# Attention scores from split queries and keys: two full-precision products per step become six single-pass ones

## The chip, the cores and the metric

The kernel runs on 1 core of one Trainium2 chip. The time is the device time in microseconds of that core, the median of three executions. Before the change: 3159.59 us (3159.53 to 3167.47).

## The reference, cut to what matters

The program computes two transformer blocks for 1024 tokens of width 1024, in float32. The change is in the second block, in its differential attention: 4 heads, each with two maps (two sets of 64-wide queries and keys), whose softmax weights are subtracted.

```python
for blk in range(t // Q_BLOCK):                    # 8 blocks of 128 queries
    start, end = blk * Q_BLOCK, (blk + 1) * Q_BLOCK
    qb = q[:, :, :, start:end].astype(jnp.float32) # (B, heads, 2 maps, 128, 64)
    kb = k[:, :, :, :end].astype(jnp.float32)
    s = jnp.einsum('bhmqd,bhmkd->bhmqk', qb, kb) * scale
    ...                                            # distance bias, causal mask
    p = jax.nn.softmax(s, axis=-1)
    a = p[:, :, 0] - lam * p[:, :, 1]
    outs.append(jnp.einsum('bhqk,bhkd->bhqd', a, vf[:, :, :end]))
```

Only the einsum that makes `s` is computed in another way by the change.

## The kernel before

Each engine has its own program in one hand-written order; semaphores join them. Most of TensorE's time goes to dense products of 128x512 columns in which float32 operands have been cut into a high part (rounded to the type fp32r) and a low part (the rest): high by high, low by high and high by low, three matmuls that each pass the array once (L436, L476 to L478). ScalarE cuts the high part of each weight tile (`WH`, L1167), GpSimd subtracts to get the low one (`WL`, L2530).

The attention stage (`pe_diff`, `act_diff`, `dve_diff`) has 32 steps n = 0 to 31: head h = n // 8, query block i = n % 8. A step works on w = 128 (i+1) keys. The step's engine order is software pipelined:

- TensorE: `scores(n)`, some pieces of dense work ("ticks": the projections of the next head and early gate products, L436), `values(n-2)` (transposes of the weights, L957), more ticks, `outs(n-3)` (products with the values, L974), and once a head the transposes of `turn` (L984).
- VectorE: `scores(n)` (L2205: add the bias, write to `PD`, take the row maximum; one instruction per map; then L2208), `weights(n-1)` (L2214 to L2218), `values(n-2)` (the copy to `AT`, L2227), and at some blocks `scale`, `norm` (a chain of 15 short instructions, then L2251) and `turn` (the copy to `SD`, L2258).
- ScalarE: `scores(n)` (the exponentials, L1468), the evacuations of the dense work (`QD`, `KD`, `VX`, `EG` by L1172) each followed by a cut of `WH` (L1167), part of `AT` (L1478), and once a head 8 squares (L1493).

Queries and keys lie transposed in `QD` and `KD`, map 0 in partitions 0 to 63 and map 1 in 64 to 127. `scores(n)` multiplies, for each map and each PSUM bank of up to 512 keys, 64 rows of float32. The profile shows each such product as two matmul records. PSUM banks are handed out in turn by `claim`, which waits until the last reader has drained them.

Of the kernel before, what the change touches and what calls it, by code (L numbers as in the profile page):

```python
# [7 lines left out]
F = mybir.dt.float32  # L8
R = mybir.dt.float32r
I32 = mybir.dt.int32  # L10
ACT = mybir.ActivationFunctionType
# [238 lines left out]
def build(nc, D, out):  # L250
    plan, order1, order2 = weight_plan()
    with ExitStack() as ctx:
        def sb(name, kb, shape, dt=F):
            return nc.alloc_sbuf_tensor_at(name, shape, dt, offset=BASE + int(kb * KB))

        def sem(name):
            return ctx.enter_context(nc.semaphore(name))
# [25 lines left out]
        ln_in, ln_ab, ln_sc, ln_g, ln_x = (sem(n) for n in (  # L283
            "ln_params_landed", "ln_stats", "ln_scaled", "ln_gained", "ln_out"))
        g_ylo2 = sem("s5_out_later_low_cut")
        t_hi, n_x = sem("token_tile_high_cut"), sem("last_tile_out")
        f_cv, f_act, f_hi, f_lo = (sem(n) for n in ("ffn_conv_begun", "ffn_activated", "ffn_mid_high_cut", "ffn_mid_low_cut"))
        xb_out, out_done = [sem(f"x_stored{t}") for t in range(8)], sem("out_stored")
# [91 lines left out]
        AT = sb("AT", 180, [128, 2, 1024])  # L380
        YD = sb("YD", 188, [128, 2, 8, 128])
        SD = sb("SD", 196, [128, 2, 1024])

        DDs = [sb("DD0", 116, [128, 1024]), sb("DD1", 120, [128, 1024])]
        YG = sb("YG", 116, [128, 8, 256])
# [520 lines left out]
        def finish(steps):  # L906
            for _ in steps:
                pass
# [16 lines left out]
        def pe_diff(e):  # L925
            def project(h):
                yield from pe_feature_steps(e, ("dq", h), "w_in_2", 128 * h)
                yield
                yield from pe_feature_steps(e, ("dk", h), "w_in_2", 512 + 128 * h)
                yield  # L930
                yield from pe_values_steps(e, ("dv", h), 1024 + 128 * h)

            def scores(n):
                h, i = diff_steps[n]
                hb, w = h % 2, 128 * (i + 1)
                if i == 0:
                    for key in (("dq", h), ("dk", h)):
                        e.wait_ge(lots[key].drained, lots[key].ndrained)
                for m in range(2):
                    rr = slice(64 * m, 64 * m + 64)  # L940
                    u = claim(e, ("ds", n, m), 1 if w <= 512 else 2)
                    for c in range(2):
                        if w > 512 * c:
                            last = e.matmul(PS[:, u.b + c, 0:min(512, w - 512 * c)], QD[rr, hb, 128 * i:128 * i + 128],  # L944
                                            KD[rr, hb, 512 * c:min(512 * c + 512, w)], start=True, stop=True)
                    last.then_inc(u.full, 1)

            def values(n):
                h, i = diff_steps[n]
                for g in range(0, i + 1, 4):  # L950
                    k = min(4, i + 1 - g)
                    u = claim(e, ("dt", n, g))
                    if g == 0:
                        e.wait_ge(d_p, n + 1)
                    for j in range(k):
                        c = 128 * (g + j)
                        last = e.transpose(PS[:, u.b, 128 * j:128 * j + 128], PD[:, n % 3, 0, c:c + 128], ident[:, :])  # L957
                    last.then_inc(u.full, 1)

            def outs(n):  # L960
                h, i = diff_steps[n]
                if i == 0:
# [13 lines left out]
                last.then_inc(d_o, 1)  # L976

            def turn(h):
                if h == 3:
                    bk.let(lots["do", 3])  # L980
                u = claim(e, ("dy", h), 2)
                e.wait_ge(d_y, h + 1)
                for i in range(8):
                    last = e.transpose(PS[:, u.b + i // 4, 128 * (i % 4):128 * (i % 4) + 128], YD[:, h % 2, i, :], ident[:, :])  # L984
                last.then_inc(u.full, 1)

            def beside(h):
                if h < 3:
                    yield from project(h + 1)
                yield from pe_early(e, BESIDE_HEAD[h])  # L990
                if h == 3:
                    yield from pe_feature_steps(e, "glr", "glr", 0)

            pe_open(e, "x2", [(("dq", 0), "w_in_2", 0), (("dk", 0), "w_in_2", 512), ((("dv", 0), "x"), "w_in_2", 1024)])
            pe_turn_values(e, ("dv", 0))
            fill = iter(())
            for n in range(36):
                if n < 32:
                    h, i = diff_steps[n]
                    if i == 0:  # L1000
                        finish(fill)
                        fill = beside(h)
                    scores(n)
                tick(fill, ticks(n)[0])
                if 2 <= n < 34:
                    values(n - 2)
                tick(fill, ticks(n)[1])
                if 3 <= n < 35:
                    outs(n - 3)
                    if diff_steps[n - 3][1] == 2 and diff_steps[n - 3][0]:  # L1010
                        turn(diff_steps[n - 3][0] - 1)
            finish(fill)
            finish(pe_gated_keys(e, 0))
            turn(3)
# [429 lines left out]
        def act_diff(e):  # L1444
            def project(h):
# [10 lines left out]
                if h < 2:  # L1456
# [3 lines left out]
                yield from act_values_steps(e, ("dv", h), VD[:, hb, :, :],  # L1460
                                            [(d_o, 8 * h - 8)] if h >= 2 else [(xb_out[4 + h], 16)])

            def scores(n):
                h, i = diff_steps[n]
                S, w = SMD[:, n % 4, :], 128 * (i + 1)
                e.wait_ge(d_s, n + 1)
                for m in range(2):
                    e.activation(PD[:, n % 3, m, 0:w], PD[:, n % 3, m, 0:w], ACT.Exp, bias=S[:, 2 + m:3 + m],  # L1468
                                 accum_out=S[:, 4 + m:5 + m]).then_inc(d_e, 1)
# [45 lines left out]
                e.activation(L(9), L(6), ACT.Ln).then_inc(lb_b, 1)  # L1515

            finish(project(0))
            fill = iter(())
            for n in range(36):
                if n == 4:  # L1520
                    bounds()
                if n < 32:
                    h, i = diff_steps[n]
                    if i == 0:
                        finish(fill)
                        fill = beside(h)
                    scores(n)
                tick(fill, ticks(n)[0])
                if 2 <= n < 34:
                    values(n - 2)  # L1530
                tick(fill, ticks(n)[1])
                if 3 <= n < 35 and diff_steps[n - 3][1] == 7:
                    take(diff_steps[n - 3][0])
                if 4 <= n and diff_steps[n - 4][1] == 7:
                    square(diff_steps[n - 4][0])
# [655 lines left out]
        def dve_diff(e):  # L2191
# [68 lines left out]
            def bounds():  # L2260
# [10 lines left out]
                e.wait_ge(lb_b, 3)  # L2271
                e.tensor_scalar(L(8), L(8), -63 * math.log(2.0), None, ALU.add).then_inc(dve, cv.up())

            e.wait_ge(cst3, 16)
            e.tensor_copy(LV[:, :, :].rearrange("p a c -> p (a c)"), LVI[:, :]).then_inc(dve, cv.up())
            e.wait_ge(dl_in, 16)
            e.tensor_tensor(DL[:, 0:64], DL[:, 0:64], DL[:, 64:128], ALU.mult).then_inc(dve, cv.up())
            then(e.tensor_tensor, DL[:, 64:128], DL[:, 128:192], DL[:, 192:256], ALU.mult)
# [3 lines left out]
            then(e.tensor_scalar, LM[:, 5:6], LM[:, 4:5], -0.2, None, ALU.add)  # L2282
            then(e.tensor_scalar, LM[:, 6:7], cols[:, C_NW:C_NW + 1], 0.8, None, ALU.mult)
            e.wait_ge(dve, cv.n)
            for n in range(36):
                if n == 4:
                    bounds()
                if n < 32:
                    scores(n)
                if 1 <= n < 33:  # L2290
                    weights(n - 1)
                if 2 <= n < 34:
                    values(n - 2)
                if 3 <= n:
                    h, i = diff_steps[n - 3] if n < 35 else (4, 0)
                    if i == 7:
                        scale(h)
                    if i == (1 if h < 4 else 0) and h:
                        norm(h - 1)
                    if i == 2 and h:  # L2300
                        turn(h - 1)
# [893 lines left out]
```

## Time and profile before

| | |
|---|---|
| median of three runs | 3159.59 us |
| profiled execution | 3164.47 us, span 3162.3 us |
| TensorE matmul busy | 3049.1 us, 96% |
| VectorE, ScalarE, GpSimd busy | 39%, 29%, 33% |
| attention stage | about 1212 to 1500 us of the span |

The span is the time from the first to the last instruction in the trace. An engine's share of busy time is a mean over all stages. Matmul durations overlap, since each includes the array's fill and drain: what a matmul costs in a stream is the distance from its start to the next one's. The chain that ended last, which is followed back from release to release, tells what a delay would cost.

### The profile page before, as it was taken

Reading aid. Unit: us, or ns where it says so; the run is one execution under the profiler, and the core shown is the slowest. Engines: PE = TensorE matmul, PEld = TensorE weight load, DVE = VectorE, ACT = ScalarE, POOL = GpSimd, SP = SyncE. Lnnn points to the kernel's source line nnn. Section 1 sums busy time; section 2 is a strip of 40 time slices with the busy share of each in tenths; the row PEclk is TensorE's granted clock in tenths of the full one; section 3 lists DMA queues with packets and bytes.
Section 4 is the critical chain, followed back from the end, with each engine's and each line's share of the span. In section 5 each row is a group of like instructions: output and inputs, shape, how many; then the busy total and the mean of one; then the engine's idle time right before and its main releaser. Section 6 shows DMA issues by size and latency. Waiting matters only on the chain.

```text
span 3162.3 us, 35710 instructions
## 1 busy us (share of the span) xinstructions
PE 3049.1 (96%) x14710; PEld 2504.5 (79%) x14710; DVE 1243.5 (39%) x2353; ACT 913.8 (29%) x1340; POOL 1046.5 (33%) x514
## 2 busy tenths in 40 slices
PE   8998999999999999999999999999999999999998
PEld 7776788888888876777777777788888788888886
DVE  8836642112122155555346544532454111112115
ACT  3223342211212134333424533433322212111111
POOL 4443345232322353111223332331223633333335
PEclk9898999999999999999999999999999999999999
DMA  6331311121111122111111111124331112111111
GB/s 208 87 113 62 95 46 48 46 67 40 54 54 40 54 64 86 53 47 61 41 34 41 54 54 48 33 80 147 127 139 41 53 54 62 52 47 47 51 43 54
DMA packets 70897, 207.62 MB, mean 66 GB/s; under 512 B 11376, under 2 KB 19968, under 8 KB 70720
## 3 DMA queue, kind: packets, MB, share of 16 engines
q1 hardware_dynamic: 70736, 205.34, 20.3%
q8 instruction: 117, 1.92, 0.2%
q14 instruction: 44, 0.36, 0.0%
HBM read 172.54 MB, written 32.77 MB: 65 GB/s over the span
## 4 chain that ended last, share of the span: by engine, by line
PE 86%; DVE 4%; ACT 3%; POOL 3%; issue 3%; DMA 0%; SPq 0%; ACTq 0%; DVEq 0%; POOLq 0%
PE PS L436 47%; PE PS L476 7%; PE PS L477 7%; PE PS L478 7%; PE PS L756 3%; PE PS L1067 3%; POOL WL L2530 2%; PE PS L944 1%; PE PS L974 1%; PE PS L502 1%; PE PS L563 1%; PE PS L859 1%; PE PS L857 1%; PE PS L858 1%; DVE s L1739 1%
## 5 line engine op out<-in xcount | busy, mean ns | idle before, releaser
L2530 POOL TENSOR_TENSOR WL<-WR,WH 128x1024 fp32r<-128x1024 f32 x241 | 580.1, 2414 | 1870.5 <-ACT WH L1167 1870.2
L436 PE MATMUL PS<-XH,WH 128*128 128x512 f32 x2176 | 690.6, 399 | 16.8 <-DVE XL L1778 9.1
L436 PE MATMUL PS<-XL,WH 128*128 128x512 f32 x2176 | 674.2, 391 | 0.0
L436 PE MATMUL PS<-XH,WL 128*128 128x512 f32 x2176 | 672.9, 390 | 0.0
L436 PEld LDWEIGHTS PS<-XH,WH 128*128 128x128 f32 x2176 | 397.2, 189 | 109.2 <-issue 25.8
L436 PEld LDWEIGHTS PS<-XH,WL 128*128 128x128 f32 x2176 | 409.8, 188 | 87.7
L436 PEld LDWEIGHTS PS<-XL,WH 128*128 128x128 f32 x2176 | 410.0, 188 | 87.3
L1167 ACT ACTIVATE WH<-WR 128x1024 fp32r<-128x1024 f32 x241 | 253.2, 1055 | 665.7 <-PE PS L478 443.4
L476 PE MATMUL PS<-WH,HH 128*128 128x512 f32 x736 | 287.2, 390 | 2.5 <-POOL HL L2562 2.5
L478 PE MATMUL PS<-WH,HL 128*128 128x512 f32 x736 | 287.0, 390 | 0.0
L477 PE MATMUL PS<-WL,HH 128*128 128x512 f32 x736 | 286.8, 390 | 0.0
L2159 DVE TENSOR_TENSOR CT<-CT,PS 128x1024 f32<-128x1024 f32 x54 | 65.9, 1221 | 459.1 <-ACT CT L1388 310.9
L2172 DVE TENSOR_TENSOR XF<-XF,PS 128x512 f32<-128x512 f32 x160 | 110.0, 687 | 313.2 <-PE PS L478 313.2
L476 PEld LDWEIGHTS PS<-WH,HH 128*128 128x128 f32 x736 | 138.5, 188 | 31.8 <-POOL HL L2562 2.9
L476 PE MATMUL PS<-WH,XH 128*128 128x512 f32 x384 | 154.5, 402 | 9.4 <-DVE XL L2026 5.4
L477 PEld LDWEIGHTS PS<-WL,HH 128*128 128x128 f32 x736 | 138.6, 188 | 28.8
L478 PEld LDWEIGHTS PS<-WH,HL 128*128 128x128 f32 x736 | 138.5, 188 | 28.9
L477 PE MATMUL PS<-WL,XH 128*128 128x512 f32 x384 | 151.7, 395 | 0.0
L478 PE MATMUL PS<-WH,XL 128*128 128x512 f32 x384 | 151.6, 395 | 0.0
L2562 POOL TENSOR_TENSOR HL<-CT,HH 128x1024 fp32r<-128x1024 f32 x54 | 129.3, 2395 | 7.6 <-ACT HH L1394 7.6
L2153 DVE SCALAR_TENSOR_TENSOR CT<-PS,cols,CT 128x1023 f32<-128x1023 f32 x22 | 28.2, 1283 | 238.3 <-ACT CT L1381 238.3
L2381 DVE COPY_PREDICATED ST<-LV,PS 128x512 f32<-128x512 uint8 x128 | 85.8, 727 | 76.1 <-PE PS L1067 75.7
(349 smaller groups left out, 3991.8 us busy)
## 6 DMA issues: line engine op xcount, KB each, us to landing
WR<-in_weights SPq DMA_DIRECT2D x241, 512.0 KB, 3.6
gates<-EG SPq DMA_DIRECT2D x18, 512.0 KB, 5.2
EI<-gates SPq DMA_DIRECT2D x18, 512.0 KB, 4.7
BR<-brbuf SPq DMA_DIRECT2D x12, 512.0 KB, 6.4
RAWX<-in_xT SPq DMA_DIRECT2D x8, 512.0 KB, 7.2
spill<-STQ SPq DMA_DIRECT2D x16, 256.0 KB, 2.2
RX<-in_x SPq DMA_DIRECT2D x8, 512.0 KB, 6.1
xbuf<-XF SPq DMA_DIRECT2D x8, 512.0 KB, 2.6
```

The costliest lines, as they stand in the source:

```text
L436: last = e.matmul(PS[:, u.b + h, :], w, x[:, k, 512 * h:512 * h + 512], start=k == 0 and w is w1 and x is xh, stop=k == nk - 1 and w is w2)
L476: e.matmul(PS[:, u.b, :], a, wh[:, k, :], start=j == 0 and k == 0, stop=False)
L477: e.matmul(PS[:, u.b, :], a, wl[:, k, :], start=False, stop=False)
L478: last = e.matmul(PS[:, u.b, :], c, wh[:, k, :], start=False, stop=j == len(vs) - 1 and k == 1)
L756: last = e.matmul(PS[:, u.b + h, :], w[:, k, :], x[:, k, 512 * h:512 * h + 512], start=k == 0 and w is wh and x is XH, stop=k == 7 and w i ...
L1067: last = e.matmul(PS[:, us[g][hh].b, 128 * (i % 4):128 * (i % 4) + 128], kl[rows[hh], c], kr[rows[hh], c], start=True, stop=True)
L1167: e.activation(WH[:, v % NSPL, :], WR[:, v % NRAW, :], ACT.Copy).then_inc(w_hi, 1)
L2159: e.tensor_tensor(X, X, bank(u, 2), ALU.mult).then_inc(u.drained, 1)
L2172: e.tensor_tensor(x, x, bank(u), ALU.add).then_inc(u.drained, 1)
L2381: e.copy_predicated(o, LV[:, n:n + 1, :].to_broadcast([128, 4, 128]), four(u)).then_inc(u.drained, 1)
L2530: e.tensor_tensor(WL[:, v % NSPL, :], WR[:, v % NRAW, :], WH[:, v % NSPL, :].bitcast(F), ALU.subtract).then_inc(w_lo, 1)
L2562: e.tensor_tensor(HL[:, v % 5, :], CT[:, v % 2, :], HH[:, v % 5, :].bitcast(F), ALU.subtract).then_inc(f_lo, 1)
```

## The change

Before each step's scores, ScalarE copies the new block of 128 keys and 128 queries to high parts (`KH`, `QH`, type fp32r), and VectorE subtracts these from `KD` and `QD` to get low parts (`KL`, `QL`, which lie where `KD` and `QD` lay). `split(n+1)` stands on ScalarE ahead of the exponentials of step n; `lows(n+1)` stands on VectorE behind the maxima of step n. TensorE's `scores(n)` claims the banks of both maps, waits for `lows(n)`, and issues for each bank three products (high queries by high keys, low by high, high by low) for map 0 and map 1 in turn. The wait for the drained projections moves from TensorE to ScalarE's `split`. The copy of the mask levels gets a semaphore of its own, since `KH` and `QH` reuse its input's place.

```diff
+        QL, KL = sb("QL", 116, [128, 2, 1024], R), sb("KL", 124, [128, 2, 1024], R)
+        KH = sb("KH", 218.75, [128, 1024], R)
+        QH = [sb("QH0", 218, [128, 128], R), sb("QH1", 205, [128, 128], R)]
...
-                for m in range(2):
-                    rr = slice(64 * m, 64 * m + 64)
-                    u = claim(e, ("ds", n, m), 1 if w <= 512 else 2)
-                    for c in range(2):
-                        if w > 512 * c:
-                            last = e.matmul(PS[:, u.b + c, 0:min(512, w - 512 * c)], QD[rr, hb, 128 * i:128 * i + 128],
-                                            KD[rr, hb, 512 * c:min(512 * c + 512, w)], start=True, stop=True)
-                    last.then_inc(u.full, 1)
+                us = [claim(e, ("ds", n, m), 1 if w <= 512 else 2) for m in range(2)]
+                e.wait_ge(d_lo, n + 1)
+                kl, ql = KL[:, hb, :], QL[:, hb, :]
+                for c in range(-(-w // 512)):
+                    k = slice(512 * c, min(512 * c + 512, w))
+                    for p, (x, y) in enumerate(((QH[n % 2][:, :], KH[:, k]), (ql[:, q], KH[:, k]), (QH[n % 2][:, :], kl[:, k]))):
+                        for m in range(2):
+                            rr = slice(64 * m, 64 * m + 64)
+                            last = e.matmul(PS[:, us[m].b + c, 0:k.stop - k.start], x[rr], y[rr], start=p == 0, stop=p == 2)
+                            if p == 2 and k.stop == w:
+                                last.then_inc(us[m].full, 1)
...
+            def split(n):                        # ScalarE
...
+                if n >= 2:
+                    read = lots["ds", n - 1 if i == 0 else n - 2, 1]
+                    e.wait_ge(read.full, read.nfull)
+                e.activation(KH[:, c], KD[:, h % 2, c], ACT.Copy)
+                e.activation(QH[n % 2][:, :], QD[:, h % 2, c], ACT.Copy).then_inc(d_hi, 1)
...
             finish(project(0))
+            split(0)
...
+                    if n < 31:
+                        split(n + 1)
                     scores(n)
...
+            def lows(n):                         # VectorE
...
+                e.wait_ge(d_hi, n + 1)
+                for L, X, H in ((KL, KD, KH[:, c]), (QL, QD, QH[n % 2][:, :])):
+                    last = e.tensor_tensor(L[:, h % 2, c], X[:, h % 2, c], H.bitcast(F), ALU.subtract)
+                last.then_inc(d_lo, 1)
...
+            lows(0)
             for n in range(36):
...
                     scores(n)
+                    if n < 31:
+                        lows(n + 1)
```

TensorE, the first step of the stage before (one row is one product of a map; w is 128):

```order
L502 MATMUL PS<-ident,VX 128x128 x3
L944 MATMUL PS<-KD,QD 128x128 [waits bank6_drained,bank0_drained]
L944 MATMUL PS<-KD,QD 128x128 [waits bank6_drained]
L436 MATMUL PS<-XH,WH 128x512 [waits weight_low_cut,bank0_drained]
L436 MATMUL PS<-XH,WH 128x512
```

The same place now (`QH_143` and `QH_144` are the two query buffers, in turn; all line numbers have moved a little):

```order
L506 MATMUL PS<-ident,VX 128x128 x3
L948 MATMUL PS<-KH,QH_143 128x128 [waits diff_block_low_cut,bank6_drained]
L948 MATMUL PS<-KH,QH_143 128x128
L948 MATMUL PS<-KH,QL 128x128 x2
L948 MATMUL PS<-KL,QH_143 128x128 x2
L440 MATMUL PS<-XH,WH 128x512 [waits weight_low_cut,bank0_drained]
L440 MATMUL PS<-XH,WH 128x512
```

Two products have become six, and the first of them waits for VectorE's subtractions.

ScalarE, the start of the stage now; before, the table load and the exponentials (L1468 then) stood directly behind the two copies to `VD`:

```order
L1171 ACTIVATE WH<-WR 128x1024 [waits bank4_full,weight_landed0]
L1436 ACTIVATE VD<-PS 128x512 [waits bank4_full,x_stored4]
L1436 ACTIVATE VD<-PS 128x512 [waits bank5_full]
L1479 ACTIVATE KH<-KD 128x128 [waits bank0_drained,bank6_drained,levels_copied]
L1480 ACTIVATE QH_143<-QD 128x128
L1479 ACTIVATE KH<-KD 128x128
L1480 ACTIVATE QH_144<-QD 128x128
L1487 ACT_TABLE_LOAD
L1487 ACTIVATE PD,SMD<-PD,SMD 128x128 [waits diff_scores_max]
```

The first split stands behind the work that ScalarE did there already, and the first scores now wait for it.

VectorE now, at step 28 (the fifth block of the last head), where the subtractions stand between the maxima (L2227 and L2230 here) and the weights of the step before (from L2236):

```order
L2227 ISA PD,SMD<-PS,AL 128x640 [waits bank6_full]
L2227 ISA SMD 128x1
L2230 TENSOR_SCALAR SMD<-SMD 128x2 [waits bank6_drained]
L2302 TENSOR_TENSOR KL<-KD,KH 128x128 [waits diff_block_high_cut]
L2302 TENSOR_TENSOR QL<-QD,QH_144 128x128
L2236 RECIPROCAL SMD<-SMD 128x2 [waits diff_exp]
L1761 TENSOR_TENSOR SMD<-SMD,LM 128x1 [waits vector_step]
```

The weights, the copy to `AT` and the norm behind them now also wait until ScalarE has split the next block.

## Rows read from the trace of the kernel before

**Rows 1.** Page: the span, and the chain that ended last by engine.

```profile
span 3162.3 us, 35710 instructions
PE 86%; DVE 4%; ACT 3%; POOL 3%; issue 3%; DMA 0%; SPq 0%; ACTq 0%; DVEq 0%; POOLq 0%
```

**Rows 2.** Chain of the stage: start us, us, engine and line, instructions.

```profile
1276.98 0.42 PE PS L944 x4
...
1282.48 0.63 PE PS L944 x4
...
1289.88 0.85 PE PS L944 x4
...
1296.99 1.06 PE PS L944 x4
...
1301.22 2.77 PE PS L436 x12
...
1304.21 1.29 PE PS L944 x8
...
1472.46 1.92 PE PS L944 x8
```

**Rows 3.** Timeline, weight loads of step 6: start, us, engine line op.

```profile
1264.79 0.31 PEld L944 LDWEIGHTS PS<-KD,QD 64*128 64x128 f32 x4
1265.32 0.20 PEld L944 LDWEIGHTS PS<-KD,QD 64*128 64x128 f32 x2 [0.23 <-issue]
1265.75 0.20 PEld L944 LDWEIGHTS PS<-KD,QD 64*128 64x128 f32 x2 [0.23 <-issue]
```

**Rows 4.** Single lines: durations in ns, min/median/max.

```profile
L2251 DVE TENSOR_TENSOR YD<-YD,SH x4: 1224/1224/1224, 1312.4 to 1510.7; 128x1024 f32<-128x1024 f32 x4
L1478 ACT ACTIVATE AT<-PS x16: 255/424/598, 1260.8 to 1494.9; 128x128 f32<-128x128 f32 x4, 128x256 f32<-128x256 f32 x4, 128x384 f32<-128x384 f32 x4, 128x512 f32<-128x512 f32 x4
L2489 DVE TENSOR_TENSOR BL<-BR,BH x12: 1211/1214/2590, 2173.7 to 2295.9; 128x1024 fp32r<-128x1024 f32 x12
```

**Rows 5.** Timeline, start of the stage.

```profile
1211.31 1.06 PE L502 MATMUL PS<-ident,VX 128*128 128x128 f32 x8 [1.21 <-ACT VX L1172]
1212.03 1.08 ACT L1432 ACTIVATE VD<-PS 128x512 f32<-128x512 f32 x2
1212.18 2.39 POOL L2530 TENSOR_TENSOR WL<-WR,WH 128x1024 fp32r<-128x1024 f32 x1 [2.98 <-ACT WH L1167]
1212.30 0.49 PE L944 MATMUL PS<-KD,QD 64*128 64x128 f32 x4
```

**Rows 6.** Timeline, step 25.

```profile
1422.65 2.38 POOL L2530 TENSOR_TENSOR WL<-WR,WH 128x1024 fp32r<-128x1024 f32 x1 [15.07 <-ACT WH L1167]
1422.76 2.30 DVE L2208 TENSOR_SCALAR SMD<-SMD 128x2 f32<-128x2 f32 x1
...
1427.96 0.64 PEld L957 LDWEIGHTS PS<-ident,PD 128*128 128x128 f32 x6 [0.49 <-DVE AT L2227]
```

**Rows 7.** Timeline, step 28.

```profile
1448.24 0.48 DVE L2216 TENSOR_SCALAR PD<-PD,SMD 128x512 f32<-128x512 f32 x1
...
1449.55 0.81 ACT L1468 ACTIVATE PD<-PD,SMD 128x640 f32<-128x640 f32 x1
```

**Rows 8.** Timeline, step 30.

```profile
1460.27 3.29 PE L944 MATMUL PS<-KD,QD 64*128 64x512 f32 x8
1460.45 1.28 DVE L2258 TENSOR_SCALAR SD<-PS,LM 128x1024 f32<-128x1024 f32 x1 [2.12 <-PE PS L984]
...
1461.79 0.29 PEld L944 LDWEIGHTS PS<-KD,QD 64*128 64x128 f32 x2 [0.37 <-DVE SD L2258]
1462.21 1.09 DVE L2205 CUSTOM_DVE_ANT_0 PD<-PS,AL 128x896 f32<-128x896 f32 x1 [0.48 <-PE PS L944]
...
1463.60 1.09 DVE L2205 CUSTOM_DVE_ANT_0 PD<-PS,AL 128x896 f32<-128x896 f32 x1 [0.28 <-PE PS L944]
...
1468.06 0.77 PE L957 MATMUL PS<-ident,PD 128*128 128x128 f32 x5 [1.54 <-ACT EG L1172]
```

**Rows 9.** Stretches: from:to, us, busy us of PE, PEld, DVE, ACT, POOL; then granted clock, DMA.

```profile
1160.00:1172.50 12.50, 9.84 (x51) 7.92 (x49) 8.45 (x35) 9.11 (x14) 9.07 (x4) 1.00 0.09 22
1172.50:1175.90 3.40, 3.35 (x8) 2.71 (x9) 1.51 (x4) 0.44 (x2) 3.40 (x3) 0.50 0.75 240
```

**Rows 10.** Timeline of TensorE around that fall of the clock.

```profile
1168.34 1.94 PE L502 MATMUL PS<-ident,XF 128*128 128x128 f32 x16 [0.44 <-POOL XF L2536]
1172.55 0.77 PE L756 MATMUL PS<-XH,WH 128*128 128x512 f32 x1 [2.28 <-DVE XL L2076]
```

More of the change, by code:

```diff
@@ L285, in build @@
         g_ylo2 = sem("s5_out_later_low_cut")
+        lv_set, d_hi, d_lo = sem("levels_copied"), sem("diff_block_high_cut"), sem("diff_block_low_cut")
         t_hi, n_x = sem("token_tile_high_cut"), sem("last_tile_out")
@@ L934, in scores @@
                 h, i = diff_steps[n]
[L935 to L938, printed above, removed]
-                for m in range(2):
-                    rr = slice(64 * m, 64 * m + 64)
-                    u = claim(e, ("ds", n, m), 1 if w <= 512 else 2)
-                    for c in range(2):
-                        if w > 512 * c:
-                            last = e.matmul(PS[:, u.b + c, 0:min(512, w - 512 * c)], QD[rr, hb, 128 * i:128 * i + 128],
-                                            KD[rr, hb, 512 * c:min(512 * c + 512, w)], start=True, stop=True)
-                    last.then_inc(u.full, 1)
+                hb, w, q = h % 2, 128 * (i + 1), slice(128 * i, 128 * i + 128)
+                us = [claim(e, ("ds", n, m), 1 if w <= 512 else 2) for m in range(2)]
[9 more added lines that the diff above has]
+                                last.then_inc(us[m].full, 1)
             def values(n):
@@ L1461, in project @@
                                             [(d_o, 8 * h - 8)] if h >= 2 else [(xb_out[4 + h], 16)])
+            def split(n):
+                h, i = diff_steps[n]
+                c = slice(128 * i, 128 * i + 128)
+                if n == 0:
+                    e.wait_ge(lv_set, 1)
+                if i == 0:
+                    for key in (("dq", h), ("dk", h)):
+                        e.wait_ge(lots[key].drained, lots[key].ndrained)
+                if n >= 2:
[3 more added lines that the diff above has]
+                e.activation(QH[n % 2][:, :], QD[:, h % 2, c], ACT.Copy).then_inc(d_hi, 1)
             def scores(n):
@@ L2272, in bounds @@
                 e.tensor_scalar(L(8), L(8), -63 * math.log(2.0), None, ALU.add).then_inc(dve, cv.up())
+            def lows(n):
+                h, i = diff_steps[n]
+                c = slice(128 * i, 128 * i + 128)
+                e.wait_ge(d_hi, n + 1)
+                for L, X, H in ((KL, KD, KH[:, c]), (QL, QD, QH[n % 2][:, :])):
+                    last = e.tensor_tensor(L[:, h % 2, c], X[:, h % 2, c], H.bitcast(F), ALU.subtract)
+                last.then_inc(d_lo, 1)
             e.wait_ge(cst3, 16)
-            e.tensor_copy(LV[:, :, :].rearrange("p a c -> p (a c)"), LVI[:, :]).then_inc(dve, cv.up())
+            e.tensor_copy(LV[:, :, :].rearrange("p a c -> p (a c)"), LVI[:, :]).then_inc(lv_set, 1)
+            e.wait_ge(lv_set, 1)
             e.wait_ge(dl_in, 16)
```

## The prediction

> **What bounds the kernel now.** I read the page's chain first: TensorE is 86% of the chain that ended last [rows 1]. Then the same chain over the attention stage (1212 to 1500 us): it goes from one group of matmuls to the next, the scores (L944) among them, so that a microsecond taken from the scores or put in front of them is one of the kernel's, as long as no other engine comes late. Last the timelines at the start of the stage and in its last head, where the chain leaves TensorE [rows 5 to 8].
>
> The reader is to see three things. The scores of a step with i = 0, 1, 2, 3 take 0.42, 0.63, 0.85 and 1.06 us, with i = 4 and 7 1.29 and 1.92 us, from their start to that of the next dense matmul [rows 2]. So 128 more keys cost both maps together 0.21 us. The weight loads of step 6 come in twos, one per map, every 0.43 us [rows 3]: the two maps run side by side already, though the program issues all of map 0 first. Alternating them therefore gives nothing by itself. And a full-height single-pass matmul of 512 columns costs 2.77 / 12 = 0.23 us [rows 2], against 0.43 us for a record of the float32 product.
>
> **TensorE's own part.** A step is now 0.10 us of first load, then per bank two records of 0.111, 0.215, 0.322 or 0.4285 us (for 128 to 512 keys), then 0.10 us until a full-height matmul may follow: this gives 0.42, 0.63, 0.85, 1.06, 1.29, 1.49, 1.71, 1.92 us, as the rows have it. After, a bank takes three single-pass records. At 512 keys I take 0.227 us each (the 0.23 above). Narrow ones cannot beat the load of 128 weight columns, 0.11 us (four loads, in two pairs one behind the other, take 0.31 us, and one pair 0.20 [rows 3]); I take 0.109 for 128 keys, 0.12 for 256, 0.174 for 384. Steps i = 0 to 7 then take 0.53, 0.57, 0.73, 0.89, 1.22, 1.25, 1.41, 1.57 us: changes of +0.11, -0.07, -0.12, -0.18, -0.07, -0.25, -0.30, -0.35, in sum -1.23 us per head and **-4.9 us** for four heads. Where map 1's banks come late, both end at the same distance from that release, so these steps save the same. No row shows single-pass products of 64 rows side by side. From one side: half a float32 record, 0.214 us at all widths in proportion, -7 us. From the other: the maps run one behind the other, which adds three records per bank, 6.5 us per head, +26 us on top of -4.9. I take the pair side by side, since the nearest row, the float32 pair [rows 3], does so.
>
> **Added work on the other engines.** Per step two ScalarE copies of 128x128 (0.26 us, the shortest of L1478 [rows 4]; with overlap about 0.5 us) and two VectorE subtractions of 128x128. L2251, the same operation at 1024 columns, takes 1.22 us [rows 4]; at about 1.05 ns a column and a fixed 0.15 us, 128 columns take 0.28 us, the two about 0.5 us. Over 32 steps that is 16 us on each, of engines that are 39% and 29% busy. ScalarE does the split while it waits for the maxima, and VectorE has several us between steps in heads 0 to 2: there it is hidden, and if that cover went it would cost up to 0.5 us a step. It shows in three places.
>
> *Start of the stage, +2.8 us.* TensorE issues the first scores at 1212.30 us. Now `split(0)` stands behind the two copies to `VD`, which end at 1213.1 [rows 5], so ScalarE is done at 1213.6. The first subtraction reads two tiles in SBUF while GpSimd's cut of `WL` runs until 1214.57 [rows 5]. In the trace a short VectorE instruction behind such a cut lasts 2.30 us until the cut ends [rows 6], and the subtraction of the same form, L2489, once takes 2.59 instead of 1.21 us [rows 4]. So 1214.6, plus 0.5, and TensorE starts at about 1215.1. Without blocking it would be 1214.1, +1.8 us; nothing bounds it below that, since the copies to `VD` come first. (The Trainium skill, page "SBUF — State Buffer", section "Who interferes with whom", states that a tensor_tensor with both inputs in SBUF contends with GpSimd's reads and that the later one waits for the whole instruction. By that rule the start costs the 2.8 us, without it 1.8; the trace agrees with the rule through L2489.)
>
> *The last head, +3.9 us.* Its steps have few ticks, so that VectorE is nearly the bound. Step 25: `L2208` sits out a GpSimd cut [rows 6], then come the weights of a 1024-wide step and the copy to `AT`, for which TensorE's transposes wait at 1427.96; the subtractions put 0.5 to 0.6 us in front of them: +0.6. Step 28: ScalarE's 8 squares end just before its exponentials at 1449.55 [rows 7]; `split(29)` now follows them, to about 1450.4 with the 0.2 us by which this place has already slipped, and `lows(29)` ends at 1451.1. The weights that began at 1448 us [rows 7] begin there, about 3 us late. Behind them stand `AT`, the norm chain, the maxima of step 29, `lows(30)`, more weights, and the copy to `SD`. This moves `SD` from ending at 1461.74 to about 1463.6. In step 30 map 1 waits for it [rows 8]; map 0 does not, and its maximum starts at 1462.21, before map 1 is done. Now both maps are claimed first, so both start at 1463.7 and end together at 1465.1: the maxima of map 0 start at 1465.2 and end with those of map 1 (1.09 us each, [rows 8]) at 1467.6 instead of 1464.9. Behind them are the exponentials, the copy to `EG`, and TensorE's transposes, which wait for it at 1468.06 [rows 8]. They slip to 1470.8: +2.7 in all, which eats the 1.2 us that steps 23 to 30 had saved and 2.7 more, together 3.9.
>
> *Steps 14 and 22, +0.3 us*: the same loss of map 0's head start, 0.75 us on VectorE, of which 0.6 has cover.
>
> **The clock.** In the old order TensorE idles 1.21 us, does 8 transposes and goes on. Now another 2.8 us of idling follow. The nearest case is at 1172.5 us: 16 transposes, 2.28 us idle [rows 10], and the granted clock is 0.50, that is 1.2 GHz, for the next 3.4 us [rows 9]. In those 3.4 us 8 matmuls run instead of 15: 7 x 0.23 = 1.6 us; a stretch may be twice as long. I count **+2.0 us**; the other end is 0.
>
> **Sum.** -4.9 + 2.8 + 3.9 + 0.3 + 2.0 = +4.1 us. On the profiled execution (3164.47 us, span 3162.3) this makes 3168.6. That execution is 4.9 us above the median of the runs shown, so I put the difference on the median: 3159.6 + 4.1 = **3163.7 us**. A measurement of this kernel can hardly tell 0.3% (9.5 us) from no change.
>
> **Rivals.**
> 1. *Cover holds everywhere but at the start* (no slip of the last head, no fall of the clock). For it: VectorE is idle 2.12 us before `SD` [rows 8], which could take up more than I let it. Against it: the squares stand directly in front of the split. -4.9 + 2.8 = -2.1: 3157.5 us.
> 2. *The single-pass maps do not run side by side.* Place: the 36 banks' worth of records of each map. Price +26 us, and it decides as soon as the third product costs more than the pass it saves, that is, if the pair takes over 0.29 us per 512 keys. For it: no row shows the pair; against it: the float32 pair [rows 3]. 4.1 + 26 = +30: 3190 us.
> 3. *Each 64-row product costs as much as a float32 record* (the single pass is not had at this height or at narrow widths). Records now cost 7.74 us per head; three for two adds half, 15.5 us in four heads, instead of saving 4.9: +24.5 us, 3184 us. If only the 128-key products (eight times three) cost a full-width float32 one, 0.43 instead of 0.109, it is +7.7 us: 3171 us.
>
> Another reading of the trace concerns whether loads hide. (The Trainium skill, page "TensorE: Matmul & The Clock Gate", section "The mechanism", states that a weight load overlaps matmuls in flight only when the row group differs. By it each added product of a pair would show 0.11 us of load, 48 of them, +5 us.) The loads of step 6 start 0.43 us apart, which is the passes alone [rows 3], so I leave this price out of the sum; it has 0.03 of the chance, inside my forecast's band.
>
> **Chances.** My forecast with its details somewhat off (3154 to 3169) 0.62; rival 1 0.17; rival 2 0.06; rival 3 in either form 0.10, half of it within 0.3% of before or little over; something not seen 0.05. Faster by over 0.3% needs more than twice what TensorE can save in my sum: 0.05. Slower by over 0.3% (above 3169): rivals 2 and 3 and the upper tail of the forecast (two slow stretches of the clock, more slips): 0.19. Within: 0.76. Range 3152 to 3177 us, with most of rival 1 and the milder half of rival 3; rivals 2 and 3 in full are left out.
>
> **What would show it.** TensorE: the step with i = 7 takes 1.57 instead of 1.92 us, with loads in twos; if it takes about 2.9, rival 2; if 2.8 with records of 0.43, rival 3. The step with i = 0 gets longer. Start: the first scores about 2.8 us later behind the transposes, the first subtraction ending with GpSimd's cut. Last head: the copy to `AT` 0.6 us later at step 25, `SD` of step 30 about 2 us later, the transposes behind `EG` 2.7 us later than the chain before. Clock: a stretch at 0.50 directly behind the first scores. The prediction is wrong if the records are not near 0.23 us at 512 columns, or if VectorE's delay reaches TensorE in heads 0 to 2.

## The result, and the profile after

The changed kernel takes 3171.46 us (median of 16 executions, 3166.32 to 3173.23), against 3159.56 us for the kernel before on the same chip (16 executions, 3149.16 to 3168.51): a ratio of 1.0033 with a 95% interval of 1.0020 to 1.0046, so about 10 us slower (6 to 15). I had forecast 3163.7 us, 4.1 more than before, with a range of 3152 to 3177. The measured time is inside the range, but above the band of 3154 to 3169 us to which I had given 0.62; times above 3169 us had 0.19.

The profiled execution took 3169.16 us against 3164.47. The page, its span and the chain by engine, which answer to [rows 1]:

```profile
span 3167.3 us, 36060 instructions
...
PE 84%; DVE 4%; ACT 4%; issue 3%; POOL 3%; DMA 0%; SPq 0%; DVEq 0%; ACTq 0%; POOLq 0%
```

TensorE's matmuls are busy 3039.5 us instead of 3049.1, and yet the span is 5.0 us longer. In the chain its share falls by two points: less of what decides the end is its work.

The chain of the stage (start us, us, engine and line, instructions) answers to [rows 2]. These are the steps with i = 0 to 4 and the first one with i = 7:

```profile
1263.16 1.59 PE PS L948 x12
...
1274.95 0.48 PE PS L948 x6
...
1280.49 0.55 PE PS L948 x6
...
1287.83 0.72 PE PS L948 x6
...
1294.78 0.90 PE PS L948 x6
...
1301.87 1.18 PE PS L948 x12
```

0.42, 0.63, 0.85, 1.06, 1.29 and 1.92 us have become 0.48, 0.55, 0.72, 0.90, 1.18 and 1.59. The weight loads of one such step (timeline of the loads) answer to [rows 3]:

```profile
1263.09 0.18 PEld L948 LDWEIGHTS PS<-KH,QH 64*128 64x128 f32 x2
1263.20 0.19 PEld L948 LDWEIGHTS PS<-KH,QL 64*128 64x128 f32 x2
1263.44 0.19 PEld L948 LDWEIGHTS PS<-KL,QH 64*128 64x128 f32 x2
1263.67 0.19 PEld L948 LDWEIGHTS PS<-KH,QH 64*128 64x128 f32 x2
```

They come in twos, 0.23 us apart at 512 keys where the float32 ones were 0.43 apart. That is what the pass of one product of 512 columns costs, so the loads of 0.19 us stay hidden and the two maps do run side by side.

The start of the stage (timeline), beside [rows 5]:

```profile
1206.32 1.07 PE L506 MATMUL PS<-ident,VX 128*128 128x128 f32 x8 [1.21 <-ACT VX L1176]
1207.04 1.08 ACT L1436 ACTIVATE VD<-PS 128x512 f32<-128x512 f32 x2
1207.20 2.35 POOL L2565 TENSOR_TENSOR WL<-WR,WH 128x1024 fp32r<-128x1024 f32 x1 [2.95 <-ACT WH L1171]
1208.02 0.31 ACT L1479 ACTIVATE KH<-KD 128x128 fp32r<-128x128 f32 x1
...
1208.63 1.07 DVE L2302 TENSOR_TENSOR KL<-KD,KH 128x128 fp32r<-128x128 f32 x1 [3.18 <-ACT QH L1480]
...
1209.61 0.28 DVE L2302 TENSOR_TENSOR QL<-QD,QH 128x128 fp32r<-128x128 f32 x1
...
1210.04 0.33 PE L948 MATMUL PS<-KH,QH 64*128 64x128 f32 x2 [2.65 <-DVE QL L2302]
```

The first scores wait 2.65 us, in the order that the prediction gave: the copies to `VD`, the split, a first subtraction that ends only 0.15 us behind GpSimd's cut (1208.63 + 1.07 = 1209.70 against 1207.20 + 2.35 = 1209.55), a second of 0.28 us.

Two stretches at half clock appear in the stage, one directly behind those scores and one in the last head. The third row is outside the stage. Columns as in [rows 9]:

```profile
1210.60:1214.00 3.40, 3.40 (x8) 2.71 (x9) 1.07 (x7) 1.28 (x6) 0.00 (x0) 0.50 0.40 149
1466.60:1470.00 3.40, 2.80 (x9) 2.45 (x10) 0.69 (x1) 1.77 (x3) 1.83 (x1) 0.50 0.00 0
1978.60:1982.00 3.40, 3.40 (x14) 3.01 (x13) 1.33 (x2) 2.51 (x5) 2.78 (x2) 0.50 0.00 1
```

The last head, beside [rows 7] and [rows 8], from the timeline of steps 28 to 30:

```profile
1440.91 0.49 PE L948 MATMUL PS<-KH,QH 64*128 64x512 f32 x2 [1.42 <-ACT EG L1176]
...
1445.20 0.40 ACT L1512 ACTIVATE JK<-YD,SH 128x128 f32<-128x128 f32 x1
...
1445.60 0.29 ACT L1479 ACTIVATE KH<-KD 128x128 fp32r<-128x128 f32 x1
...
1446.12 0.29 DVE L2302 TENSOR_TENSOR KL<-KD,KH 128x128 fp32r<-128x128 f32 x1 [2.01 <-ACT QH L1480]
...
1447.99 0.55 DVE L2249 COPY AT<-PS 128x384 f32<-128x384 f32 x1
...
1448.64 0.50 PE L948 MATMUL PS<-KH,QH 64*128 64x512 f32 x2 [1.37 <-issue]
...
1453.49 0.95 DVE L2227 CUSTOM_DVE_ANT_0 PD<-PS,AL 128x768 f32<-128x768 f32 x1
1453.63 0.66 PE L961 MATMUL PS<-ident,PD 128*128 128x128 f32 x4 [0.72 <-DVE SMD L2227]
...
1458.70 1.28 DVE L2280 TENSOR_SCALAR SD<-PS,LM 128x1024 f32<-128x1024 f32 x1 [1.40 <-PE PS L988]
...
1461.73 1.09 DVE L2227 CUSTOM_DVE_ANT_0 PD<-PS,AL 128x896 f32<-128x896 f32 x1 [1.74 <-PE PS L948]
...
1462.75 1.09 DVE L2227 CUSTOM_DVE_ANT_0 PD<-PS,AL 128x896 f32<-128x896 f32 x1
...
1467.20 1.33 PE L961 MATMUL PS<-ident,PD 128*128 128x128 f32 x5 [2.66 <-ACT EG L1176]
```

The reader should follow the delay downwards. The last of the squares (L1512) starts at 1445.20. Only behind it, at 1445.60, comes the split, and VectorE had idled 2.01 us for it. Its weights come late, so the copy to `AT` ends at 1448.54, and the scores of step 29 start 0.10 us later: TensorE stood still 1.37 us ahead of them, for a bank that this copy drains. "issue" there means that the trace names no releaser; but the transposes that the copy reads and one map of the scores of step 29 raise the same semaphore when they end, so they use the same bank. Then the transposes behind those scores wait 0.72 us for the first of VectorE's maxima of step 29. At `SD` it is VectorE that waits for TensorE (1.40 us on L988), and both maps of step 30 start when `SD` is done.

### The profile page after: what moved, and what is told of

It is laid out like the page before. It is cut to its first block, busy times and chain, and to the rows that moved or that the text cites. A ratio compares the mean times of both kernels' runs of the same rounds, so it can differ in the third digit from the quotient of the medians.

```text
span 3167.3 us, 36060 instructions
## 1 busy us (share of the span) xinstructions
PE 3039.5 (96%) x14806; PEld 2511.2 (79%) x14806; DVE 1257.3 (40%) x2417; ACT 926.4 (29%) x1404; POOL 1049.2 (33%) x514
## 4 chain that ended last, share of the span: by engine, by line
PE 84%; DVE 4%; ACT 4%; issue 3%; POOL 3%; DMA 0%; SPq 0%; DVEq 0%; ACTq 0%; POOLq 0%
PE PS L440 46%; PE PS L480 7%; PE PS L481 7%; PE PS L482 7%; PE PS L760 3%; PE PS L1071 3%; POOL WL L2565 2%; PE PS L948 1%; PE PS L978 1%; PE PS L506 1%; PE PS L567 1%; PE PS L863 1%; PE PS L861 1%; PE PS L862 1%; DVE s L1761 1%
```

## Where the difference arises

I read the same marks in each trace: the last dense product ahead of the stage, the first dense product behind `scores(0)` (start), step 24 (heads 0 to 2), and the end of the stage. The sums are worked out from start times of the same matmuls; those taken for the last two marks start some 0.5 us ahead of the first product of step 24 and 0.8 us ahead of the first dense one behind the stage. "Half clock" is the time at 0.50 within the stage. The last three columns are differences to before in us: the stage; everything from the stage's first mark to the end of the span, against the mean of the four traces of before; and the whole kernel by its ratio.

| kernel | start | heads 0-2 | last head | half clock | stage | from the stage on | kernel |
|---|---|---|---|---|---|---|---|
| before (4 traces) | 3.0 | 208.2 | 79.0 | 0 | 0 | 0 | 0 |
| after | 5.8 | 206.3 | 83.4 | 6.8 | +5.2 | +9.2 | +10.4 |
| after again | 6.1 | 206.8 | 83.6 | 10.2 | +6.3 | +7.3 | +7.9 |
| work without saving | 6.0 | 210.4 | 81.6 | 6.8 | +7.8 | +6.7 | +6.3 |
| first split alone | 6.0 | 210.4 | 79.0 | 6.8 | +5.3 | +4.1 | +4.1 |
| maps one after the other | 6.2 | 211.6 | 81.4 | 6.8 | +8.9 | +10.5 | +8.2 |
| the three edits together | 3.1 | 209.5 | 79.4 | 0 | +1.8 | +3.8 | +4.1 |
| earlier first split | 3.1 | 204.8 | 83.6 | 3.4 | +1.2 | +2.6 | +0.3 |
| split ahead of the squares | 6.1 | 206.8 | 79.9 | 6.8 | +2.6 | +4.2 | +1.3 |
| both, still alternating | 3.1 | 204.8 | 81.5 | 3.4 | -0.9 | +0.4 | 0.0 |
| float32 alternated | 3.0 | 208.9 | 80.3 | 0 | +1.9 | +2.0 | +1.3 |

The last column is uncertain by 3 to 5 us either way. The stage explains it within 2.5 us in all but one row, that of the first trace after the change.

That the first two spans differ by just the stage's 5 us is chance. The program ahead of the stage has the same 5440 matmuls in every kernel, and the stage's first mark falls between 1201 and 1211 us, at 1204.7 after the change and at 1209.7 before: this part was 5.0 us shorter. What follows, counted from the first dense product behind the stage, was 4.8 us longer (1666.3 against 1661.5 us). It too has the same matmuls everywhere, and what moves it is mostly stretches at half clock. It takes 1660.3, 1661.5, 1661.5 and 1665.9 us in the four traces of before and 1663.3 to 1666.3 in the seven with single-pass scores.

## The experiments

**Work without saving** (e_work). The splits, subtractions and waits stay; the scores are the two float32 products again. The low parts are written over the high ones and used by nothing.

```diff
-                e.wait_ge(d_lo, n + 1)
...
+                    if m == 0:
+                        e.wait_ge(d_lo, n + 1)
...
-                for L, X, H in ((KL, KD, KH[:, c]), (QL, QD, QH[n % 2][:, :])):
-                    last = e.tensor_tensor(L[:, h % 2, c], X[:, h % 2, c], H.bitcast(F), ALU.subtract)
+                for X, H in ((KD, KH[:, c]), (QD, QH[n % 2][:, :])):
+                    last = e.tensor_tensor(H, X[:, h % 2, c], H.bitcast(F), ALU.subtract)
```

> All the splitting stays (two ScalarE copies and two VectorE subtractions a step, TensorE's wait for them), but TensorE multiplies the unsplit float32 queries and keys, map 0 first, as before the change; the subtractions write over the high parts, which nothing reads. My theory (single-pass products save about 4.9 us in the attention stage, the added work costs 2.8 us at its start and about 4 us in the last head, and the clock adds some): the stage is 5 us longer than with the change and 9 to 11 us longer than before. Rival A (the products are what costs, the splitting is hidden): the stage takes what it did before. Rival B (what was lost lies outside the stage, where half-clock stretches fall): the stage differs from before by under 3 us.

Measured: ratio 1.0020 (1.0011 to 1.0028). The stage is 7.8 us longer than before, less than the 9 to 11 expected, and 1.5 to 2.6 us longer than with the change instead of 5. Heads 0 to 2 take 210.4 us, the same as in the next kernel, which has no work there: the added work is hidden in them. In the last head it costs 2.6 us and not 4: this kernel keeps map 0's lead and has no half-clock stretch there.

**First split alone** (e_start_only). As e_work, but `split`, `lows` and the wait for n = 0 only.

```diff
-                    if n < 31:
-                        split(n + 1)
...
-                    if n < 31:
-                        lows(n + 1)
...
+                    if m == 0 and n == 0:
+                        e.wait_ge(d_lo, 1)
```

> The kernel before, with only the first step's split and subtractions and TensorE's wait for them; no other step is split, all products are float32 as before. My theory: the first scores start about 3 us later behind the transposes, a stretch of half clock follows them in the profile, and the stage is 4 to 5 us longer than before. Rival (TensorE's later waits absorb the delay): under 1.5 us longer.

Measured: ratio 1.0013 (0.9999 to 1.0026). The start costs 3.0 us and the last head nothing. Heads 0 to 2 are 2.2 us longer, through 6.8 us at half clock behind the first scores: the one wait brings two costs.

**Maps one after the other** (e_seq). All three products of map 0, then those of map 1, each with its own claim.

```diff
-                for c in range(-(-w // 512)):
...
+                for m in range(2):
+                    rr = slice(64 * m, 64 * m + 64)
+                    u = claim(e, ("ds", n, m), 1 if w <= 512 else 2)
```

> The change, but map 0's products are all issued ahead of map 1's, with the banks of map 1 claimed only then. My theory (the two maps run side by side in whatever order they are issued, and map 0's lead is worth something where map 1's banks come late): a step with i = 7 takes 1.6 us as with the change, the weight loads come in twos, and the last head's step 30 has its first maximum 1 us earlier; the time is 0 to 2 us below the change's. Rival (only alternation makes them run side by side): the step with i = 7 takes 2.9 us, and the time is about 26 us above.

Measured: ratio 1.0026 (1.0015 to 1.0036). The expectation (1.6 us at i = 7, and a time at or below the change's) was wrong: the stage is 2.6 to 3.7 us longer than with the change. TensorE's timeline at step 7, then three pieces of the chain:

```profile
1271.81 0.50 PE L949 MATMUL PS<-KH,QH 64*128 64x512 f32 x1
1272.15 0.39 PE L949 MATMUL PS<-KH,QL 64*128 64x512 f32 x1
1272.38 0.39 PE L949 MATMUL PS<-KL,QH 64*128 64x512 f32 x1
1272.38 0.61 PE L949 MATMUL PS<-KH,QH 64*128 64x512 f32 x2
...
1273.65 0.39 PE L949 MATMUL PS<-KL,QH 64*128 64x512 f32 x1
```

```profile
1271.88 2.15 PE PS L949 x12
...
1284.24 0.49 PE PS L949 x6
...
1289.79 0.55 PE PS L949 x6
```

Map 1's first product starts at 1272.38, together with map 0's third, 0.57 us after map 0's first. The step ends alone with map 1's last products: 2.15 us instead of 1.59. Steps with i = 4 to 7 take 1.75, 1.83, 1.98 and 2.15 us (1.18, 1.24, 1.43 and 1.59 when alternating), those with i = 0 to 3 are as short as before. With six products of map 0 ahead of it map 1 comes late; with three, or with the four records of the float32 version, it does not. In heads 0 to 2 this costs 4.8 us (211.6 against the 206.8 of c_after, which has the same 6.8 us at half clock there). In the last head it takes some 2 us less than alternating (81.4 against 83.4 and 83.6), but without the half-clock stretch that both alternating traces have in it.

**The three edits together** (e_best): e_seq with the next two.

> The change with three mends: the first split stands on ScalarE behind the copy to KD instead of behind the copies to VD; in the steps with squares the next split stands ahead of them; map 0's products are issued first, its banks claimed alone. My theory: all of the start's 3 us and its half-clock stretch go, and most of the last head's 4 us, so the stage is 3 to 5 us shorter than before the change and about 9 shorter than with it. Rival (VectorE's subtractions themselves, 0.5 us a step, carry the loss of the last head): the stage is within 1 us of before.

Measured: ratio 1.0013 (1.0000 to 1.0026). The stage is 1.8 us longer than before, where 3 to 5 us shorter was expected. The start (3.1 us) and the last head (79.4) are repaired; the late map 1 costs 4.7 us in heads 0 to 2 (209.5 - 204.8). What map 0's lead gives back in the last head, less what the late map 1 costs there, is 0.5 us (79.4 against the 79.9 of e_squares, neither with a half-clock stretch in it).

**After again** (c_after), unchanged.

> The change as it is, once more, beside the others on the same chip. My theory: the stage costs about 5 us more than before in the profile, and where half-clock stretches fall outside the stage differs from one execution to the next; the time is 4 to 12 us above before. Rival (the stage's loss seen in the first profile was an accident of the clock): the stage is within 2 us of before.

Measured: ratio 1.0025 (1.0012 to 1.0039). Start and last head agree with the first trace within 0.4 us. The stretch behind the first scores is 6.8 us long instead of 3.4 and costs 2.0 us instead of 1.5 (206.8 and 206.3 against 204.8 of the kernel below that has none).

**Earlier first split** (e_start). `split(0)` directly behind the evacuation of the keys.

```diff
                 act_evac(e, lots["dk", h], KD[:, hb, :], 2)
+                if h == 0:
+                    split(0)
...
             finish(project(0))
-            split(0)
```

> The change with one mend: the first split stands on ScalarE behind the copy to KD instead of behind the copies to VD. My theory: the first scores follow the transposes as before the change, the half-clock stretch there goes, and by the end of head 2 the stage is 3 to 4 us ahead of before; the last head still gives back about 4; the stage comes out 4 to 5 us shorter than with the change. Rival (GpSimd's cut blocks the subtraction wherever it stands, or the delay is only moved): under 1.5 us shorter.

Measured: ratio 1.0001 (0.9986 to 1.0016). Its timeline, where the split stands 5.7 us ahead of the first scores:

```profile
1198.98 0.30 ACT L1481 ACTIVATE KH<-KD 128x128 fp32r<-128x128 f32 x1
...
1202.81 0.29 DVE L2303 TENSOR_TENSOR KL<-KD,KH 128x128 fp32r<-128x128 f32 x1
...
1203.66 1.06 PE L506 MATMUL PS<-ident,VX 128*128 128x128 f32 x8 [1.21 <-ACT VX L1176]
...
1204.66 0.33 PE L948 MATMUL PS<-KH,QH 64*128 64x128 f32 x2
```

The scores follow the transposes without a wait, the clock does not fall there, and heads 0 to 2 show the saving bare: 208.2 - 204.8 = 3.4 us. The last head still costs 4.6. The stage is 4.0 to 5.1 us shorter than with the change, as expected.

**Split ahead of the squares** (e_squares). In steps 12, 20 and 28 the next split is issued before the squares instead of behind them.

```diff
-                    if n < 31:
+                    if n < 31 and n not in (12, 20, 28):
                         split(n + 1)
...
                 if 4 <= n and diff_steps[n - 4][1] == 7:
+                    if n < 31:
+                        split(n + 2)
                     square(diff_steps[n - 4][0])
```

> The change with one mend: in steps 12, 20 and 28 the split of the next block stands ahead of the squares instead of behind them. My theory (the squares in front of the split delay the subtractions, and by them VectorE's chain up to the copy to SD): SD of step 30 ends 2 us earlier against the scores of step 27 than with the change, and the last head gives back 1.5 to 2.5 us less. Rival (the subtractions themselves fill VectorE in the last head): under 0.7 us less.

Measured: ratio 1.0004 (0.9992 to 1.0017). The last head is 0.9 us longer than before instead of 4.4. It is 3.5 to 3.7 us shorter than with the change, more than the 1.5 to 2.5 expected, because no half-clock stretch falls in it. The chain runs on TensorE from step 28 to step 30 without the wait ahead of step 29; what stays is the 1.50 us until `SD` is done, ahead of the scores of step 30:

```profile
1438.25 1.26 PE PS L948 x12
...
1444.61 1.24 PE PS L948 x12
...
1448.85 0.66 PE PS L961 x4
...
1453.82 1.50 issue
1455.31 1.48 PE PS L948 x11
```

How far each mark lies behind the kernel before, in us, counted from the start of step 24 in each trace (1421.62 before, 1417.41 after, 1414.75 here):

| mark | before, at | after | split ahead of the squares |
|---|---|---|---|
| end of the scores, step 28 | 1446.01 | +0.3 | +0.4 |
| end of the scores, step 29 | 1452.64 | +1.5 | +0.1 |
| transposes behind the scores of step 29 | 1455.43 | +2.4 | +0.3 |
| end of the scores, step 30 | 1463.57 | +2.2 | +0.1 |
| transposes behind `EG`, step 30 | 1468.06 | +3.4 | +1.2 |
| end of the scores, step 31 | 1474.38 | +4.4 | +0.9 |

So the place behind the squares costs 2.1 us (3.35 - 1.23 at the transposes behind `EG`). The other 1.2 us stay in both: they arise in step 30, where both maps now end together and the maxima of both follow. The half-clock stretch adds some 1.3 us by the end of step 31 (4.4 - 3.4, and 0.3 that the step itself saves); this kernel has none there.

**Both, still alternating** (e_best2).

> The change with both mends, the first split early and the splits ahead of the squares, and the two maps alternating as in the change. The run with map 0 first showed that with two banks per map the maps then overlap only from the third product on (2.15 us instead of 1.59 at i = 7), so alternation stays. My theory: the stage is 2 to 5 us shorter than before the change and 7 to 9 us shorter than with it; the kernel is 0 to 5 us faster than before. Rival (the lost lead of map 0 carries the last head's loss): it gives back 3 us there all the same, and the stage is within 1 us of before.

Measured: 3159.31 us, ratio 1.0000 (0.9985 to 1.0015). The stage is 0.9 us shorter than before. This is the best form of the changed kernel, and it only draws level: 3.4 us saved in heads 0 to 2, 2.5 lost in the last head, where a half-clock stretch has come back. The rival of the expectation described this better than my theory of 2 to 5 us: about 1.2 of the 2.5 us are map 0's lost lead, the rest the stretch.

**Float32 alternated** (e_alt32). The kernel before with both claims first and the float32 products of the two maps in turn, nothing split.

```diff
+                us = [claim(e, ("ds", n, m), 1 if w <= 512 else 2) for m in range(2)]
+                for c in range(-(-w // 512)):
+                    k = slice(512 * c, min(512 * c + 512, w))
+                    for m in range(2):
```

> The kernel before with one part of the change alone: the banks of both maps are claimed first and the float32 products of the two maps alternate bank by bank; nothing is split. My theory (they ran side by side anyway, and all that this part does is to take away map 0's lead where map 1's banks come late): steps with i = 7 stay at 1.92 us, and in the last head the transposes behind EG come 0.5 to 1.5 us later against the scores of step 27; the stage is 0.5 to 2 us longer than before. Rival (alternation is a gain by itself): the steps with i = 4 to 7 get shorter by 0.2 us or more.

Measured: ratio 1.0004 (0.9992 to 1.0016). The step with i = 7 keeps its 1.92 us, and the stage is longer by 0.6 us in heads 0 to 2 and 1.3 in the last head. For the float32 products the alternation gains nothing and costs map 0's lead: the transposes behind `EG` in step 30 come 1.3 us later than before, counted from step 24, nearly the 1.2 us that both kernels of the table above keep. TensorE's wait there:

```profile
1465.33 0.77 PE L958 MATMUL PS<-ident,PD 128*128 128x128 f32 x5 [2.66 <-ACT EG L1173]
```

That wait is 2.64 to 2.67 us in all six traces in which the maps alternate, and 1.53 to 1.55 in the eight in which map 0 goes first. So the long wait comes from the two maps going together and not from the splitting. The half-clock stretch of the last head goes with it: four of the six traces have one, none of the eight.

**The kernel before, three times more** (c_before1 to c_before3), one execution each, for what varies outside the stage.

> The kernel before, unchanged, for another profile. My theory: half-clock stretches behind TensorE's waits at about 1975 and 2072 us, which the first profile of before did not have and all seven of the changed kernels had at least one of, fall in some executions of before too, so that the last 5 us of the difference between the first two profiles are an accident of the execution and no effect of the change. Rival (the change brings them): no profile of before shows them.

> As the run before: one more profile of the unchanged kernel. My theory: some half-clock stretch near 1975 or 2072 us in one of the three. Rival: in none.

> As the two runs before: one more profile of the unchanged kernel. My theory: the attention stage from the last product ahead of it to 1500 us takes the same to 0.3 us in all profiles of before, except for half-clock stretches in it. Rival: it varies by over 1 us without them.

Measured: 3168.86, 3159.47 and 3165.49 us. The stage takes 290.22 to 290.24 us in all three (290.32 in the first trace), without a half-clock stretch. Outside it, c_before1 has what only the changed kernel had in the first pair of traces:

```profile
1978.10:1981.50 3.40, 3.40 (x12) 2.83 (x11) 1.65 (x2) 2.83 (x6) 2.47 (x2) 0.50 0.00 0
2077.10:2080.50 3.40, 3.40 (x17) 3.31 (x16) 0.54 (x1) 1.73 (x4) 3.40 (x2) 0.50 0.25 100
```

Two of four traces of before have this pair of stretches. The first trace of the changed kernel loses 1.9 and 1.6 us there against a trace of before that has none.

## Why the prediction came out as it did

The sign and most of the terms held, but the difference is 10.4 us (6.3 to 14.5) in the first measurement and 7.9 (3.8 to 12.3) in the second, against 4.1 forecast. That the time is inside the range is owed to the range's upper part, which I had kept for rivals that did not come true. By its steps:

- *TensorE's own part, -4.9 us: right.* Forecast 0.53, 0.57, 0.73, 0.89, 1.22, 1.25, 1.41, 1.57 us for i = 0 to 7; measured 0.48, 0.55, 0.72, 0.90, 1.18, 1.24, 1.43, 1.59. In heads 0 to 2 this and the +0.3 of steps 14 and 22 should make -3.4, and e_start shows -3.4, though the two parts lie a little apart from mine: the measured steps give -3.9, and e_alt32 shows 0.6 us for the lost lead there. Rival 2 and rival 3 in full are ruled out by the loads 0.23 us apart, rival 3's milder form by the 0.48 us at i = 0. (Two slips that change nothing in the sum: each map has 48 bank products and not 36, and half float32 records would give -7.7 us and not -7.)
- *Added work hidden in heads 0 to 2: right*, by e_work against e_start_only.
- *Start, +2.8: right*, 2.8 and 3.1 us in the two traces, 0.1 with the earlier split. The blocked subtraction took 1.07 us instead of 0.28. (The rule of the Trainium skill, page "SBUF — State Buffer", section "Who interferes with whom", that the later of the two waits for the other's whole instruction, agrees with that row.)
- *Clock, +2.0: right where I put it* (1.5 and 2.0 us), *missed in the last head*, where TensorE waits 2.66 us for `EG` and the clock falls again: some 1.3 us in no term of mine. The wait grew from 1.54 us by map 0's lost lead, which I had priced as a delay but not as a wait that the clock answers to.
- *Last head, +3.9, or +2.7 with what its steps save: right in size, partly wrong in the way.* Measured is 4.4, without the clock about 3.1 (4.4 - 1.3), so rival 1 is out. The squares were the larger cause, 2.1 us, as e_squares shows, map 0's lead the other, 1.2 us, and step 25 slips by 0.4 us (its transposes start at 1424.15, against 1427.96 in [rows 6] less 4.21; forecast 0.6). But I let VectorE's delay reach TensorE only at `SD` in step 30. It came earlier, through banks: 1.2 us at the scores of step 29 and 0.9 at the transposes behind them. At `SD` VectorE waited for TensorE's transposes (1.40 us on L988): `SD` ended late because TensorE was already late, not because VectorE was. I had followed VectorE's queue and not asked at each of its reads whose bank it was holding.
- *"Alternating them therefore gives nothing by itself": wrong as a general statement.* It holds for the float32 products (e_alt32), which is all that [rows 3] could show. With three products per bank and two banks per map it fails: without alternation steps i = 4 to 7 would have lost 0.55 to 0.6 us each (e_seq), and the change's saving with it.
- *The sum:* -3.4 (heads 0 to 2) + 2.8 + 1.5 (clock) + 4.4 = +5.3 us in the stage, against +4.1 forecast and +5.2 and +6.3 in the traces. The rest of the medians' +10.4 and +7.9 us lies behind the stage as far as the traces show: from the stage on they are 9.2 and 7.3 us longer than the mean of before. My sum had no term there. Why it is longer there is not settled. Executions of before spread over 19 us, its four traces differ by up to 5.7 us from the stage on, and stretches of the clock outside the stage come and go from one execution to the next. Near 1979 and 2075 us eight of the ten traces with a changed program show both stretches and two show one, against both in two of the four of before; whether the change makes them more frequent stays open with such counts.

## What to carry to other kernels

A cheaper product is worth only what stays after the waits that its preparation puts into the queues: here 4.9 us were to be had, and one split placed behind a block of squares and one placed behind unrelated copies took more than that, until both were moved. Price such an edit at each queue, ask of each late read which PSUM bank it still holds, and count a new or a longer wait of TensorE, here of 2.65 us, as possibly costing the clock too. Claiming two maps' banks together is an edit of its own, with a price of its own. When two half-height products share the array, see that the second one's first instruction is not far behind the first's.

## What the runs showed of the hardware

- Two 64-row products side by side cost 0.23 us per 512 columns as single passes, 0.43 us per float32 record. The step with 128 keys takes 0.48 us against 0.42: three loads one behind the other, 0.11 us apart, decide there. (The Trainium skill, page "TensorE: Matmul & The Clock Gate", section "The mechanism", states in its list of what overlaps that a load overlaps matmuls in flight only when the row group differs; above that list the same section also lets a load into the background weight buffer be pulled ahead. The trace disagrees with the first sentence: the loads of 0.19 us belong to row groups that are at work, and the products stay 0.23 us apart.)
- How far the second row group may stand behind the first in the program matters: four float32 records ahead of it cost nothing (1.92 us in either order), six single-pass products delay it by 0.57 us.
- The clock fell to 0.50 behind a wait of TensorE of 2.65 us at the start in all six traces that have this wait, and in none of the eight without it. In the last head it fell behind one of 2.66 us in four traces; but behind the same wait in e_squares (2.65 us) and e_alt32 (2.66 us) it stayed up. The same kernel showed a stretch of 3.4 us once and 6.8 the other time. So one profile tells that such a stretch is possible, not that it will be there.
